# mLSTM head norm: the normalised rows written by ScalarE with scale and bias, VectorE left with the product of mean and rstd

## What is computed

```python
hs = h_f + flip(h_b)                                   # (B, heads, T, 128)
mu = jnp.mean(hs, axis=-1, keepdims=True)
var = jnp.mean(jnp.square(hs - mu), axis=-1, keepdims=True)
hn = ((hs - mu) * lax.rsqrt(var + LN_EPS)).transpose(0, 2, 1, 3).reshape(B, T, D_MODEL)
hn = hn * head_g
out = (jax.nn.sigmoid(o) * hn) @ w_out
```

## Time and profile before

| what | value |
|---|---|
| runs | 1438.93, 1436.56, 1438.68 us |
| median | 1438.68 us |
| span of the profiled execution | 1437.3 us |
| TensorE busy (products) | 1358.2 us, 94% |
| VectorE busy | 941.3 us, 65% |
| ScalarE busy | 772.2 us, 54% |
| GpSimd busy | 215.2 us, 15% |
| mean DMA rate | 253 GB/s |
| loop of the heads | about 668 to 757 us of the span |

### The profile page before, as it was taken

How to read it: one execution, slowest core, us unless ns; L and a number is a source line. 1 busy time by engine, 2 the same in 40 slices (tenths; PEclk the granted TensorE clock), 3 DMA queues, 4 the chain that set the end, 5 groups by cost and what they waited for, 6 DMA issues and landing times.

```text
span 1437.3 us, 21263 instructions
## 1 busy us (share of the span) xinstructions
PE 1358.2 (94%) x6883; PEld 1114.3 (78%) x6883; DVE 941.3 (65%) x1234; ACT 772.2 (54%) x1172; POOL 215.2 (15%) x283
## 2 busy tenths in 40 slices
PE   6999889999999989999889899999999999999986
PEld 2766468999999979987557687877888888888864
DVE  0425567363333475323886798768999999999877
ACT  1323565233323353332434686557888888888763
POOL 1010000080000002303330564204200000000100
PEclk9999999999999999999999999999999999999998
DMA  9786664459444524437656699978999999999991
GB/s 337 239 298 230 219 225 123 135 195 364 123 119 128 146 57 123 131 121 252 235 211 208 197 378 366 313 221 282 368 370 370 371 368 368 370 369 369 372 370 60
DMA packets 271285, 362.98 MB, mean 253 GB/s; under 512 B 17006, under 2 KB 225164, under 8 KB 271084
## 3 DMA queue, kind: packets, MB, share of 16 engines
q1 hardware_dynamic: 258602, 321.58, 67.6%
q0 software_dynamic: 12368, 40.44, 7.6%
q10 hardware_dynamic: 242, 0.01, 0.0%
HBM read 340.15 MB, written 20.76 MB: 251 GB/s over the span
## 4 chain that ended last, share of the span: by engine, by line
PE 74%; DVE 9%; SPq 5%; DMA 4%; issue 4%; ACT 4%; POOL 0%; DVEq 0%; ACTq 0%
PE PS L2330 20%; PE PS L508 14%; PE PS L2338 10%; PE PS L484 7%; PE PS L486 7%; PE PS L485 7%; SPq L2076 4%; PE PS L633 2%; DMA BIG<-in_moe_w_down 1%; ACT whi L2093 1%; DVE wlo L2097 1%; DMA BIG<-in_poolm 1%; PE PS L2298 1%; DMA raw<-in_moe_w_gu 1%; DMA BIG<-in_moe_w_gu 1%
## 5 line engine op out<-in xcount | busy, mean ns | idle before, releaser
L460 DVE TENSOR_TENSOR wlo<-raw,whi 128x1024 fp32r<-128x1024 f32 x130 | 168.2, 1319 | 224.2 <-ACT whi L457 223.9
L2097 DVE TENSOR_TENSOR wlo<-BIG,whi 128x1024 fp32r<-128x1024 f32 x216 | 266.6, 1252 | 37.8 <-ACT whi L2093 33.5
L2093 ACT ACTIVATE whi<-BIG 128x1024 fp32r<-128x1024 f32 x216 | 227.6, 1059 | 42.5 <-PE PS L2330 21.0
L2330 PE MATMUL PS<-whi,Hh 128*128 128x512 f32 x560 | 223.9, 400 | 0.6 <-DVE Hl L2182 0.4
L2097 DVE TENSOR_TENSOR wlo<-raw,whi 128x1024 fp32r<-128x1024 f32 x162 | 196.6, 1225 | 33.8 <-ACT whi L2093 30.7
L2330 PE MATMUL PS<-wlo,Hh 128*128 128x512 f32 x560 | 218.3, 390 | 0.0
L484 PE MATMUL PS<-Hh,whi 128*128 128x384 f32 (+1 forms) x624 | 208.4, 334 | 2.8 <-DVE wlo L460 1.5
L486 PE MATMUL PS<-Hh,wlo 128*128 128x384 f32 (+1 forms) x624 | 207.1, 332 | 0.0
L485 PE MATMUL PS<-Hl,whi 128*128 128x384 f32 (+1 forms) x624 | 206.9, 332 | 0.0
L2330 PE MATMUL PS<-whi,Hl 128*128 128x512 f32 x504 | 197.1, 391 | 0.0
L2093 ACT ACTIVATE whi<-raw 128x1024 fp32r<-128x1024 f32 x162 | 171.1, 1059 | 46.6 <-PE PS L2338 18.0
(11 more groups left out here) (411 smaller groups left out, 1951.1 us busy)
## 6 DMA issues: line engine op xcount, KB each, us to landing
raw<-in_moe_w_gu SPq DMA_DIRECT2D x252, 256.0 KB, 6.9
BIG<-in_moe_w_gu SPq DMA_DIRECT2D x252, 256.0 KB, 7.2
raw<-in_ada_w SPq DMA_DIRECT2D x96, 512.0 KB, 5.9
BIG<-in_moe_w_down SPq DMA_DIRECT2D x90, 512.0 KB, 8.0
raw<-in_ffn_w_gu SPq DMA_DIRECT2D x44, 512.0 KB, 5.2
raw<-in_moe_w_down SPq DMA_DIRECT2D x36, 512.0 KB, 8.1
raw<-in_w_in_c SPq DMA_DIRECT2D x32, 512.0 KB, 4.2
scr_tok<-BIG POOLq DMA_DIRECT2D x27, 512.0 KB, 10.6
```

What stands on the lines that cost most here:

```text
L460: self.eng.tensor_tensor(wlo[:, s, :], raw[:, s, :], whi[:, s, :].bitcast(f32), ALU.subtract).then_inc(lo_made, 1)
L2093: act.activation(whi[:, slot(v), :], moe_raw(v), ACT.Copy).then_inc(hi_made, 1)
L2097: dve.tensor_tensor(wlo[:, slot(v), :], moe_raw(v), whi[:, slot(v), :].bitcast(f32), ALU.subtract).then_inc(lo_made, 1)
L2330: last = pe.matmul(PS[:, 6 * b + c % 2, :], lhs, wt[:, s, 512 * k:512 * k + 512], start=(q == 0 and k == 0 and i == 0), stop=(q == 3 and k ...
```

## The change

ScalarE, right behind its Exp, waits for a small product from VectorE and writes the three tiles of `hn` by an Identity activation each, with `hrs` as its scale and `hmv[:, :, 0]` as its bias. VectorE, in place of the three tensor_scalar, waits for the Exp and overwrites the means by `-mean * rstd` (one scalar_tensor_tensor on 128x3). The semaphore `hrstd` now counts two for a head. The wait for `ht_turned` (the head before has been transposed, so `hn` may be written) goes to ScalarE too.

```diff
@@ act_mixer1
                     act.wait_ge(hvar, h + 1)
                     ch.step(act.activation(hrs, hmv[:, :, 1], ACT.Ln, bias=C("small", 128, 0, 1)))
                     act.activation(hrs, hrs, ACT.Exp, scale=-0.5).then_inc(hrstd, 1)
+                    act.wait_ge(hrstd, 2 * h + 2)
+                    if h:
+                        act.wait_ge(ht_turned, h)
+                    for t in range(TT):
+                        last = act.activation(hn[:, t, :], hs[:, t, :], ACT.Identity, scale=hrs[:, t:t + 1],
+                                              bias=hmv[:, t, 0:1])
+                    last.then_inc(hn_made, 1)
                 if i < NM:
                     ada.units(2)
@@ dve_mixer1
                         if u == NM - 1:
                             sp_.upto(U_OUTC + 1)
-                        dve.wait_ge(hrstd, h + 1)
-                        if h:
-                            dve.wait_ge(ht_turned, h)
-                        for t in range(TT):
-                            last = dve.tensor_scalar(hn[:, t, :], hs[:, t, :], hmv[:, t, 0:1], hrs[:, t:t + 1],
-                                                     ALU.subtract, ALU.mult)
-                        last.then_inc(hn_made, 1)
+                        dve.wait_ge(hrstd, 2 * h + 1)
+                        dve.scalar_tensor_tensor(hmv[:, :, 0], hmv[:, :, 0], -1.0, hrs, ALU.mult, ALU.mult).then_inc(hrstd, 1)
```

## The result

The changed kernel takes 1451.6 us (four runs, 1451.06 to 1453.0), the kernel before 1438.43 us (four runs). The ratio is 1.0095, 95% interval 1.0081 to 1.011: slower by 13.2 us, where 10.8 were forecast.

A forecast was written before the change was run, and what follows sets the result against it. No engine was full; a chain of waits, mostly through VectorE and crossing to ScalarE at the norm, bounded the loop. 9.0 + 1.1 + 0.7 = 10.8 us on 1438.7 gave 1449.5 us, range 1445 to 1453.5.

The forecast's parts named there:

- What bounds the loop: Loop of the heads: no engine full, a chain of waits mostly through VectorE, crossing to ScalarE at the norm.
- rival 1: VectorE's relief decides at the clamp: 1.1 us saved a head, 8 us over seven, 1430.7 us; chance 0.04.
- What the removal brings: At the clamp: removing VectorE's three tensor_scalar brings at most the slack behind the decay, 0.68 us over seven heads.
- The shift of the decay, 9.0 us: ScalarE's queue: decay begins 1.38 us later a head, behind trip and activations; 9.66 over seven less 0.68 slack.
- The small product, 1.1 us: VectorE's new product held beside GpSimd's L1751: excess 0.43 us in two heads, 0.13 in two.
- What costs nothing: `hn`'s transposes stay covered, the last head has 1.0 us cover, DMA is unmoved, GpSimd's state copies move with the decay.
- The clock, 0.7 us: TensorE in the loop: one more fall to half clock that hurts, 0.7 us; bounds 0 and 4.2.
- The sum: Whole kernel: 9.0 + 1.1 + 0.7 = 10.8 us slower, 1449.5 us; chance 0.75.
- Half absorbed: Loop: TensorE and loads get ahead while VectorE waits, leaving some 5 us, 1443.7 us; chance 0.06.
- The clock: a small part: Rival: TensorE falls to half clock in all seven heads, between clamp and numerators, 14.3 us, 1453.0 us; chance 0.12.
- what was to be looked for: Signs in the changed profile, among them VectorE's 3.0 us wait for the decay growing to some 14.

The follow-up runs named there:

- run 2: The changed kernel with the next unit's decay moved before the Ln, into ScalarE's wait for the statistics: 1434.9 us, ratio 0.9986.
- run 3: The kernel before, VectorE still writing `hn`, with the next unit's decay made before the Ln: 1438.2 us, ratio 1.0003.
- run 1: The changed kernel with the next unit's decay moved between the Exp and the wait for the small product: 1441.4 us, ratio 1.0019.
- run 5: The changed kernel with GpSimd's multiplication for the next forward unit held until `hn` is written: 1450.3 us, ratio to the kernel before 1.0079.
- run 4: The kernel before, with three idle activations writing an unused tile between Exp and decay, `hn` still on VectorE: 1448.2 us, ratio 1.0074.
- run 7: The changed kernel with decay before the Ln, GpSimd's multiplication held and 8 clock products ahead of the transposes: 1432.1 us, ratio 0.9962.
- run 8: The changed kernel with early decay, held multiplication, no clock products, and the `gate_bc` copy in the third head before the Ln: 1431.1 us, ratio 0.9958.
- run 9: As run 8, with 4 products ahead of the transposes except in head 2: 1428.7 us, ratio to the kernel before 0.994.
- run 6: The changed kernel with 8 products for the clock in TensorE's idle time ahead of each transpose of `hn`: 1455.2 us, ratio 1.0115.
- run 10: As run 5, with 8 products ahead of the transposes except in head 2: 1449.4 us, ratio 1.0087.

## Why the prediction was right, point by point

- **What bounds the loop.** Right: no engine but a chain, and ScalarE's decay as what the clamp meets next. But the earlier trace rows were misread, and rival 1 was argued down with them in part. The seven waits of 3.0 us for the decay were not those of the norm. They are the clamps of the other units, where the decay stands behind `Hh`: runs 2 and 3, in which the norm's decay is early, still have them (3.0 us, 7 times). That `hn` and decay end together was rightly read from the timeline; the wait view did not show it, since a tie leaves no wait.
- **What the removal brings:** at most the slack of 0.68 us. Right: in run 1, where the decay stands as before, the clamp gained 1.1 us in sum (12.0 less 10.9), of which 0.5 in head 2, where the decay now stands ahead of the copy too; the other 0.6 is the slack.
- **The shift of the decay, 9.0 us.** Measured without the long products, in run 5: 21.8 less 12.0, 9.8 us. The term mis-sized is the activation: three hold the queue 1.17 us (756.79 to 757.96), not 1.06, where L1601, with its input in PSUM, held it for 0.35 each. Run 4 points at the source: its activations have the same kind of scale and bias columns as L1601 but read SBUF, and take 477 to 481 ns, where L1601 takes 449 to 472. The changed kernel's line, ns min/median/max:

```profile
L1613 ACT ACTIVATE BIG<-BIG x24: 478/480/496, 681.4 to 769.6; 128x128 f32<-128x128 f32 x24
```

  The Trainium skill ("ScalarE: Activation LUTs", section "ACT is a hardware spline evaluator") gave 0.48 and, by the same sum, an estimate of 9.7 us. The trace agrees with it, and here it was better than the nearest row.
- **The small product, 1.1 us.** Measured 1.3 (run 5): 0.69 in two heads and 0.39 in one. Right in size; it was held for longer than the tensor_scalar had been, see below.
- **What costs nothing.** The transposes and the last head stayed covered: from the last Ln to TensorE's output projection it is 1.13 us in both. That the copy of `gate_bc` shifts by the same and no more held too, since the decay was later still; by an estimate from run 7, whose head 2 took 13.50 us from Ln to Ln, 1.40 of it the added products, where the changed kernel's took 12.69, the chain of that copy lay only some 0.6 us behind.
- **The clock, 0.7 us.** Behind the clamp the loop lost 1.5 in the profile (heads 1 and 4 each 0.8 longer, head 3 0.1 shorter). Five falls began in the loop, not two, and two more than before cost time, where one was taken. But a fall was priced at 0.7 of slower products: these cost 0.47 in head 4, and 0.35 came from VectorE's add, held beside a GpSimd multiplication that the slower products had delayed. Of the 1.5, 0.8 is products and 0.7 two held adds, a cost that the prediction did not have. That its term came near the first part is in part luck.
- **The sum.** 10.8 forecast; 12.6 in the profiled loops: the missing 1.8 are 0.8 from the activations, 0.2 from the product and 0.8 behind the clamp. All three terms were too small, so no error hid another. The medians are 13.2 apart; the other 0.6 is within what single executions differ by.
- **The rivals.** VectorE's relief, the case of a faster kernel, failed on this change and came true in runs 2, 7, 8 and 9, where its condition (a decay made ahead of the activations) was met. Half absorbed: nothing was. The clock: a small part.
- Of what was to be looked for, VectorE's wait for the decay grew by 16.7 us, not by 11, because each of the seven is a whole new wait of 2.3 us, or 2.8 in head 2, beside the old seven: the shift of the decay and the work that VectorE no longer has there.

## What to carry to other kernels

Work moved to an idle engine is queued in that engine's program: look at what stands behind it there and who waits for that, not at its busy share. When two engines end together, shortening one brings nothing until the other's work is moved too, and moving first what has its inputs early (here a decay that could fill ScalarE's wait for the statistics) turns a loss of 13 us into a gain of 2 to 8. An engine off the chain still counts: here GpSimd's multiplication, started by TensorE's products, held a VectorE operation on the chain whenever it came to stand beside it. After each such step the next chain is a few tenths or a microsecond behind; plan for it, and keep work meant to hold the clock off places where its engine comes late.

## What the runs showed of the hardware

- A VectorE operation on 128x3 with both inputs in SBUF, usually 0.16 us, was held until GpSimd's multiplication was over: in head 0 of the changed kernel until 681.38, where that ended at 681.35 (680.63 + 0.72). The Trainium skill ("SBUF — State Buffer", section "SBUF: two separate sides") says so, for the whole of the instruction; the trace agrees here, better than with L1676 before. In head 2 of run 2 (and in the same head of runs 1 and 6) it was held 1.01 us though it stands in the record 0.25 us ahead of the multiplication:

```profile
698.97 0.19 POOL L1755 COPY BIG<-BIG 128x1 f32<-128x1 f32 x1
699.11 0.72 POOL L1757 TENSOR_TENSOR BIG<-wlo,BIG 128x256 f32<-128x256 f32 x1
```

  The product began at 698.86 and ended at 699.88 in the chain. Whether GpSimd's operation really began earlier than its record, or something else held the product, stays open.
- The add on 128x384 (L1676, in the changed kernel L1683), 0.56 us with nothing beside it, took 0.91 when GpSimd's multiplication of 0.73 us had begun 0.25 ahead of it, eleven times in the kernel before, the changed kernel and run 5, and 0.75 once when it had begun 0.41 ahead.
- Identity with scale and bias from a column holds ScalarE's queue for 0.39 us on 128x128 from SBUF, 0.48 to its end. VectorE's tensor_scalar on the same took 0.34 in the median: at this size the move made the work itself a little longer.
- TensorE's clock fell to the half level twice in the loop of the kernel before, five times in the changed one and six times in run 5. With products put into TensorE's idle time it fell four times in run 6, once in run 10 and not at all in runs 7 and 9; without such products it fell once in run 8, whose heads are shorter. What a fall costs depends on where it lands: 0 to 0.8 us, the held add counted in.
